# Moving the weight tiles and five activation tiles of a two-stack transformer kernel to other byte positions in SBUF

## The reference, cut

```
act = gelu(einsum('td,ted->te', xb, u[eid]))       # x times every u row
out = einsum('te,ted->td', g * act, v[eid])        # weighted sum of v rows
h + (silu(gate) * up) @ w_down                     # SwiGLU, second stack
```

## The kernel before, in words

| tile | place modulo 512 |
|---|---|
| `wH`, `wL` | 128 |
| `hnH`, `hnL`, `memH`, `memL`, `wgtH`, `wgtL` | 128 |
| `pr_hH/L`, `ff_aH/L`, `pr_qH/L`, `ml_nH/L` | 128 |
| `att_OTH/L`, `od_hH/L`, `od_yH/L` | 192 |
| `ycatH/L` | 416 |

## Time and profile before

### The profile page before, as it was taken

One profiled execution on the slowest core, in us unless ns is written; L12 is line 12 of the kernel. 1 busy time (PEld: TensorE's weight loads), 2 busy tenths in 40 slices (PEclk: granted clock), 3 DMA queues, 4 the chain that ended last, 5 costly groups with the idle time before them and its releaser, 6 DMA issues.

```text
span 2841.9 us, 57248 instructions
## 1 busy us (share of the span) xinstructions
PE 2768.2 (97%) x19552; PEld 2600.4 (92%) x19552; DVE 2048.3 (72%) x4430; ACT 1454.4 (51%) x2378; POOL 179.7 (6%) x141
## 2 busy tenths in 40 slices
PE   7999999999999999989999999999999999999998
PEld 7999899999988888979999999988888889999998
DVE  8657987886567677876698888566677876666665
ACT  5455445444455555555544444455555565446444
POOL 0004000000000000000275000000000000000000
PEclk9999999999999999999999999999999999999999
DMA  5445565455766665424456554676666525553454
GB/s 191 177 152 180 202 221 203 170 180 191 239 247 242 241 242 187 148 82 156 151 179 217 184 181 168 211 251 242 244 241 240 190 90 178 188 217 125 173 190 178
DMA packets 140452, 546.19 MB, mean 192 GB/s; under 512 B 15785, under 2 KB 81593, under 8 KB 83617
## 3 DMA queue, kind: packets, MB, share of 16 engines
q1 hardware_dynamic: 63216, 455.38, 44.4%
q10 hardware_dynamic: 73728, 67.14, 7.6%
q0 software_dynamic: 3376, 21.88, 2.0%
HBM read 505.53 MB, written 40.91 MB: 192 GB/s over the span
## 4 chain that ended last, share of the span: by engine, by line
PE 80%; DVE 12%; DMA 3%; ACT 2%; issue 2%; POOL 2%; SPq 0%; DVEq 0%; ACTq 0%
PE bank L796 24%; PE bank L797 23%; PE bank L798 23%; PE bank L1016 4%; DVE wL L551 3%; DMA ring<-in_w_stream 2%; POOL wL L551 2%; PE bank L917 1%; PE bank L937 1%; ACT wH L540 1%; PE bank L928 1%; DVE pr_m L1973 0%; DVE pr_eq L1969 0%; DVE pr_eq L1971 0%; PE bank L893 0%
## 5 line engine op out<-in xcount | busy, mean ns | idle before, releaser
L551 DVE TENSOR_TENSOR wL<-ring,wH 128x1024 fp32r<-128x1024 f32 x809 | 988.3, 1224 | 632.9 <-ACT wH L540 623.0
L540 ACT ACTIVATE wH<-ring 128x1024 fp32r<-128x1024 f32 x864 | 907.4, 1055 | 407.4 <-DMA ring<-in_w_stream 230.2
L796 PE MATMUL bank<-hnH,wH 128*128 128x256 f32 x3528 | 1020.0, 289 | 21.4 <-DVE wL L551 14.6
L797 PE MATMUL bank<-hnL,wH 128*128 128x256 f32 x3528 | 1002.4, 284 | 0.0
L798 PE MATMUL bank<-hnH,wL 128*128 128x256 f32 x3528 | 1002.3, 284 | 0.0
L796 PEld LDWEIGHTS bank<-hnH,wH 128*128 128x128 f32 x3528 | 680.8, 193 | 30.4 <-issue 15.1
L797 PEld LDWEIGHTS bank<-hnL,wH 128*128 128x128 f32 x3528 | 681.2, 193 | 0.5 <-issue 0.2
L798 PEld LDWEIGHTS bank<-hnH,wL 128*128 128x128 f32 x3528 | 680.4, 193 | 0.0
L796 PE MATMUL bank<-wH,wgtH 128*128 128x512 f32 x1024 | 398.5, 389 | 0.0
L797 PE MATMUL bank<-wL,wgtH 128*128 128x512 f32 x1024 | 398.4, 389 | 0.0
L798 PE MATMUL bank<-wH,wgtL 128*128 128x512 f32 x1024 | 398.3, 389 | 0.0
(11 more groups left out here) (411 smaller groups left out, 3530.6 us busy)
## 6 DMA issues: line engine op xcount, KB each, us to landing
ring<-in_w_stream SPq DMA_DIRECT2D x432, 1024.0 KB, 4.9
act_parked<-act_out ACTq DMA_DIRECT2D x256, 128.0 KB, 2.6
act_in<-act_parked ACTq DMA_DIRECT2D x256, 128.0 KB, 2.8
sw_bias<-in_c_swa POOLq DMA_DIRECT2D x1, 4096.0 KB, 15.5
relb_rows<-rel_table POOLq DMA_DIRECT2D x1, 2048.0 KB, 9.7
h_parked<-h POOLq DMA_DIRECT2D x2, 1024.0 KB, 5.9
h_back<-h_parked POOLq DMA_DIRECT2D x2, 1024.0 KB, 6.2
od_relb<-relb_rows POOLq DMA_DIRECT2D x2, 1024.0 KB, 7.6
```

The costliest lines, as they stand in the source:

```text
L540: eng.activation(wH[:, b % NBUF, :], raw(b), ACT.Copy).then_inc(w_high, 1)
L551: eng.tensor_tensor(wL[:, b % NBUF, :], raw(b), wH[:, b % NBUF, :].bitcast(F32), ALU.subtract).then_inc(w_low, 1)
L796: pe.matmul(dst, lh, rh, start=start, stop=False, skip_group_check=True)
L797: pe.matmul(dst, lh, rl, start=False, stop=False, skip_group_check=True)
```

## The change

The change alters where tiles lie and nothing else: the instructions, their number, their order and their waits stay as they are.

1. `vec`, `lbv`, `snk` and `rb` (544, 96, 64 and 32 bytes, 736 together) are allocated ahead of `wH` and `wL` and no longer behind them. Both weight tiles and `act_out`, `con` and `iww` behind them move up: `wH` and `wL` from 128 to 352 modulo 512, `con` (identity, ones, iota) from 160 to 352.
2. A `stage` entry may name a number of float32 elements to skip. The tile is then allocated that much longer and starts that many elements later. Both tiles of five pairs get one: `att_OT` 2 (8 bytes), `ff_a` 4 (16), `ycat` 6 (24), `od_y` 10 (40), `pr_h` 12 (48). With the rounding to 32 bytes the low tile of each pair moves further than the high one.
3. Tiles allocated behind the lengthened ones in the same `stage` call move by the same rounding (`mem_raw` by 64 bytes, `od_neg` and all the `hg_` tiles by 128).

Worked out from the sizes and the rounding, the places modulo 512 after the change are: `wH/wL` 352, `hn`, `mem`, `wgt`, `pr_q` and `ml_n` 128 as before, `od_h` 192 as before, `att_OT` 200 and 232, `ycat` 440 and 472, `pr_h` 176 and 240, `od_y` 232 and 296, `ff_a` 144 and 176.

```diff
+                held = []
+                for name, shape, dt, *skip in wanted:
+                    if skip:
+                        flat = scope.enter_context(nc.sbuf_tensor(name, [P, skip[0] + shape[0] * shape[1]], dt))
+                        held.append(flat[:, skip[0]:].rearrange("p (a b) -> p a b", b=shape[1]))
+                    else:
+                        t = scope.enter_context(nc.sbuf_tensor(name, [P] + list(shape), dt))
+                        held.append(t[tuple([slice(None)] * (len(shape) + 1))])
+                return held
...
-            ("att_PT", [DEEP, 256], F32), ("att_O", [2, 1024], F32), ("att_OTH", [8, 256], F32R),
-            ("att_OTL", [8, 256], F32R))
+            ("att_PT", [DEEP, 256], F32), ("att_O", [2, 1024], F32), ("att_OTH", [8, 256], F32R, 2),
+            ("att_OTL", [8, 256], F32R, 2))
...
-                ("poolL", [4, 256], F32R), ("ycatH", [8, 256], F32R), ("ycatL", [8, 256], F32R),
+                ("poolL", [4, 256], F32R), ("ycatH", [8, 256], F32R, 6), ("ycatL", [8, 256], F32R, 6),
...
-        _, pr_hH, pr_hL = stage(("pr_h_before", [8192], F32), ("pr_hH", [DC, T], F32R), ("pr_hL", [DC, T], F32R))
+        _, pr_hH, pr_hL = stage(("pr_h_before", [8192], F32), ("pr_hH", [DC, T], F32R, 12), ("pr_hL", [DC, T], F32R, 12))
...
-                ("od_relb", [16, 256], F32), ("od_yH", [8, 256], F32R), ("od_yL", [8, 256], F32R),
+                ("od_relb", [16, 256], F32), ("od_yH", [8, 256], F32R, 10), ("od_yL", [8, 256], F32R, 10),
...
-            ("ff_aH", [FC, 256], F32R), ("ff_aL", [FC, 256], F32R))
+            ("ff_aH", [FC, 256], F32R, 4), ("ff_aL", [FC, 256], F32R, 4))
...
         ring = sb("ring", [P, SLOTS, 2 * BLK])
+        vec, lbv, snk, rb = sb("vec", [P, NVEC]), sb("lbv", [P, 24]), sb("snk", [P, 16]), sb("rb", [32, 8])
         wH, wL = sb("wH", [P, NBUF, BLK], F32R), sb("wL", [P, NBUF, BLK], F32R)
```

More of the change, by code:

```diff
@@ L351, in stage @@
             with ExitStack() as scope:
-                held = [scope.enter_context(nc.sbuf_tensor(name, [P] + list(shape), dt)) for name, shape, dt in wanted]
-                return [t[tuple([slice(None)] * (len(w[1]) + 1))] for t, w in zip(held, wanted)]
+                held = []
[7 more added lines that the diff above has]
+                return held
         AR = 32768 - DC * T
@@ L434, in build_stacks @@
         root_sb, mem_root = act_out[:, 0, :], act_out[:, 1, :]
-        vec = sb("vec", [P, NVEC])
         con = sb("con", [P, NCST])
         iww = sb("iww", [P, DC, 8])
-        snk = sb("snk", [P, 16])
-        rb = sb("rb", [32, 8])
         slotT = sb("slotT", [P, 3, T])
@@ L442, in build_stacks @@
         eps = small[:, 80:81]
-        lbv = sb("lbv", [P, 24])
         psum = [ctx.enter_context(nc.psum_tensor(f"bank{i}", [P, 512], F32)) for i in range(ALL_BANKS)]
```

## The result

The changed kernel takes 2849.3 us (median of 13 runs, 2843.5 to 2856.2) against 2838.8 for the kernel before on the same chips. The ratio is 1.0031 with a 95% interval of 1.0019 to 1.0042, so it is slower, by about 0.3%. The forecast was 2797 us, with a range that ended at 2838.

What follows compares the result with a forecast made beforehand. The prediction took PE, busy 97% of the span, as the bound, through matmul spacing. Gains of 31.5 + 7.4 + 2 = 41 us took the 2838.2 us median to 2797 us, range 2764 to 2838.

Steps and rivals of the forecast that it cites:

- PE bounds the kernel and the spacing is its price: Most of the span: time is matmul count times spacing, with 13.4 ns excess per matmul whatever the width.
- The distance of the moving from the stationary place decides: All products: distance modulo 512 sets the spacing; 0 gives 120.1 ns, 64 gives 117.9, 288 gives 116.4.
- The row of `ycatL`: ycatL at distance 288 before the change: 116.4 ns per matmul, taken as the forecast for hn and mem.
- The MLA rows: MLA projections: ml_n stays at 128 while stationary slices vary; 117.5 ns each, read as showing the stationary place matters.
- 256 columns, 31.5 us: hn and mem over the weights: 9,000 matmuls gain 3.5 ns each, about 2,000 of 10,968 left out for waits.
- 512 columns, 7.4 us gained: Moving weights over wgt, mem, hn and ml_n: some 3,360 matmuls, 2.2 ns less each, bounds -12 to +15 us.
- the slow phase: 512-column form just after a restart: nine steps at 231.1 ns each, used as that form's upper end.
- `ff_a`, 2 us; the other tiles 0, up to 5: ff_a gains 1.9 ns on 3 x 352 matmuls; att_OT, ycat, od_y, pr_h taken 0, bound 5 us.
- Feeders and other engines, 0: ACT and DVE writing weights, other tiles' offsets, and DMA: no cost from the move, taken 0.
- The slower rival: 512-column form settles at 231 ns (+15 us) and hn slows likewise (+40 us): 2893 us, chance 0.09.
- No effect of places: Rival for all PE products: differences between tiles come from something else in the loops; 2838 +- 4, chance 0.06.
- the moving place alone: Rival: only the moving tile's own place counts, hn and mem stay at 120.1 ns; 2823 to 2838, chance 0.09.

Runs made afterwards that it cites:

- the bench: Separate kernel that copies x and only issues both product forms at chosen distances, nothing else running: 113.3 to 122.1 ns for 256 columns, 226.7 to 234.1 for 512.
- the half feed: Kernel before, with DVE and POOL filling only the first 512 of 1024 columns of each wL block after the first four: 2799.5 us, ratio 0.9854.
- hn_32: Kernel before with small tiles moved so hn is 32 bytes behind the weights modulo 256, weights still at 128: 2825.7 us, ratio 0.9955.
- skips_only: Kernel before plus only the bytes in front of the five tile pairs, weights still at 128: 2840.1 us, ratio 0.9997.
- w_only: Kernel before plus only the weights' move to 352, without the bytes in front of the five tile pairs: 2851.5 us, ratio 1.0032.
- half-feed pair: Half of each wL block's split dropped after the first four, on the kernel before and on hn_32: 2799.5 us (0.9854) and 2772.3 us (0.9767).
- the first bench: Copy-only kernel issuing both product forms, stationary pair at 128 for 256 columns, distances upward from 0 to 504: 120.0 ns at 0, 116.7 at 32, 113.3 at 64.

## Why the prediction was wrong, point by point

- *PE bounds the kernel and the spacing is its price.* Right, but the waits were read as 24 us that stay as they are, and they grew with every gain. The price itself was read as 13.4 ns "whatever the width". That holds for 256 and 512 columns. The key scores in the same trace, with 128 columns, are 1.34 us / 12 = 112 ns apart where 128 columns take 53.3:

```profile
246.75 0.27 PE L797 MATMUL bank<-wL,pr_qH 128*128 128x128 f32 x1
...
248.09 0.27 PE L797 MATMUL bank<-wL,pr_qH 128*128 128x128 f32 x1
```

  The sum does not use this.
- *The distance of the moving from the stationary place decides.* Right, but the distance is not all. The period was wrong, 256 bytes and not 512; it did no harm here, since the bench gave 116.7 at 288 and 32 alike. The row of `ycatL` that carried the forecast was partly luck. Its spacing from all starts is 116.7, and in the kernel before with the half feed, where no place differs, the same tile stood at 117.8. The MLA rows did not show what was read from them: their loads have 96 columns and not 128, their distances of 0 and 128 modulo 256 gave 120.0 and 118.7 in the bench, and their mean stayed between 117 and 118 after the weights had moved (117.8 before, 117.2 after).
- *256 columns, 31.5 us.* The spacing was right, the term less so. The regular intervals fell by 32 us on `hn` and 1 on `mem`, but by 10,600 matmuls at 3.1 ns and not 9,000 at 3.5, so the sum agrees partly by luck. The allowance of 2,000 matmuls was meant for the waits, and it was too small: alone, in `hn_32`, the gain on `hn` was worth 13 us of time.
- *512 columns, 7.4 us gained.* **The first step that failed.** It measured 22 us lost, a term off by 29 us and in its sign. I leaned on "every distance seen other than 0 has been cheaper than 0". That was a statement on the form with 256 moving columns, and I carried it to a form whose optimum turned out to be distance 0. The row that should have warned was the slow phase, which I took as an outer bound of 231.1; the bench shows 233.3 as the ordinary value and 226.7 as the exception. The upper bound itself was too low by 2.2 ns.
- *`ff_a`, 2 us; the other tiles 0, up to 5.* Right: 3.4 us gained on `ff_a`, 2 to 3 lost on the others, together within the noise. `skips_only` has other distances; the fitting comparison is `w_only` with the change, 2851.5 and 2849.3 us.
- *Feeders and other engines, 0.* **The second step that failed.** It cost 15 us of waits and 5 of half clock. I looked for places where PE would be slowed by DMA in the long stages, which held (the v stage kept 0.65 of the DMA's share), and not at the chain in which each block of `wL` passes through ACT and DVE between their other duties. The half-feed pair put its price at half of the gain on `hn`.
- *The slower rival.* It named the deciding form, the wide one settling in a slow phase, but coupled it to a slow `hn` and so gave it 2893 us and a chance of 0.09. The wide form alone, with `hn` as forecast, at its measured 22 us lost, would have been 2797 + 29 = 2826, and only with 20 us of waits and half clock 2846. Neither failed step alone turns the sign.
- *No effect of places* fell with the first bench, and *the moving place alone* with `hn`, whose own place did not change. The latter rival was priced with 1,056 matmuls for the five tiles, which is `ff_a` alone; they hold 2,424.

## What to carry to other kernels

Where PE is saturated, take the spacing of each matmul form from count and starts, and look at places of the moving against the stationary tile; a form with 256 moving columns and one with 512 need different distances, so measure each form before a shared operand is moved. A gain per matmul is worth only what the feeder of the next block can follow. To see how much of a gain is lost to it, repeat the pair, without and with the edit, with the feeder made cheaper.

## What the runs showed of the hardware that was not expected

- The spacing of these `float32r` products with a weight load each runs from 113.3 to 122.1 ns for 256 columns and from 226.7 to 234.1 for 512, by the distance modulo 256 bytes and the cycle it falls into, with all other engines idle and the clock at 1.00.
- At some distances there is more than one steady cycle, with all places the same: 113.4 or 117.8 ns at 192 and 116.7 or 117.9 at 32. At 112 the fast one was reached in both benches after some ten matmuls.
- A gap of 2.7 us in a saturated stretch was followed, about a microsecond later, by 15 intervals of 214 ns, at the lower level of the clock. Against 116.7 ns that is about another 1.5 us.
